# In three norms of a transformer kernel the GpSimd engine multiplies every second part by the inverse root, and the scalar engine makes the modulated row from it

## The reference, cut to what matters

```
h = x * rsqrt(mean(x^2) + eps) * g * (1 + scale) + shift
x_new = x_new + gt2 * squared_relu_mlp(h, w1, w2)
```

## Time and profile before

| | us |
|---|---|
| three runs | 1960.61, 1961.11, 1963.31 |
| median | 1961.11 |
| the profiled execution | 1964.24 |
| its span | 1962.4 |
| PE busy | 1858.6 (95%) |
| DVE busy | 1176.7 (60%) |
| ACT busy | 901.2 (46%) |
| POOL busy, 156 instructions | 103.7 (5%) |

### The profile page before, as it was taken

How to read it: one execution, slowest core, us unless ns; L and a number is a source line. 1 busy time by engine, 2 the same in 40 slices (tenths; PEclk the granted TensorE clock), 3 DMA queues, 4 the chain that set the end, 5 groups by cost and what they waited for, 6 DMA issues and landing times.

```text
span 1962.4 us, 28960 instructions
## 1 busy us (share of the span) xinstructions
PE 1858.6 (95%) x11398; PEld 1484.1 (76%) x11398; DVE 1176.7 (60%) x2039; ACT 901.2 (46%) x1552; POOL 103.7 (5%) x156
## 2 busy tenths in 40 slices
PE   7999899988999899999998999999899899999999
PEld 6889754445977554788787888888778548999999
DVE  5778732335633566578976666666743555676665
ACT  6564422115554577632235433232374576455443
POOL 0000012221000000001100000000000000000000
PEclk9999999999999999999999999999999999999999
DMA  9546799997522002155633444556533013554553
GB/s 335 182 146 220 290 397 412 413 415 284 172 86 80 22 1 86 56 181 193 208 114 132 159 160 131 190 182 205 194 108 102 22 43 108 176 190 151 183 183 130
DMA packets 199255, 345.48 MB, mean 176 GB/s; under 512 B 14096, under 2 KB 158736, under 8 KB 185936
## 3 DMA queue, kind: packets, MB, share of 16 engines
q1 hardware_dynamic: 177024, 284.88, 41.6%
q0 software_dynamic: 21952, 57.97, 8.7%
q10 hardware_dynamic: 144, 0.79, 0.1%
HBM read 392.86 MB, written 1.05 MB: 201 GB/s over the span
## 4 chain that ended last, share of the span: by engine, by line
PE 77%; DVE 9%; DMA 6%; ACT 4%; issue 2%; SPq 0%; DVEq 0%; ACTq 0%
PE PS L861 20%; PE PS L863 19%; PE PS L862 19%; PE PS L987 3%; PE PS L1236 3%; DMA SCR<-in_w_exp 3%; DVE JUNK L2219 2%; PE PS L1005 2%; DMA ring<-in_w_exp 2%; PE PS L1022 2%; DVE CR L1912 2%; PE PS L1219 1%; PE PS L1264 1%; DMA LC<-in_w_mod 1%; PE PS L993 1%
## 5 line engine op out<-in xcount | busy, mean ns | idle before, releaser
L1912 DVE TENSOR_TENSOR CR<-ring,CR 128x1024 fp32r<-128x1024 f32 x328 | 400.2, 1222 | 294.7 <-ACT CR L1457 282.6
L861 PE MATMUL PS<-HX,CR 128*128 128x256 f32 (+1 forms) x1512 | 507.7, 336 | 20.9 <-DVE HX L1961 11.4
L862 PE MATMUL PS<-HX,CR 128*128 128x256 f32 (+1 forms) x1512 | 495.6, 328 | 0.0
L863 PE MATMUL PS<-HX,CR 128*128 128x256 f32 (+1 forms) x1512 | 495.5, 328 | 0.0
L1457 ACT ACTIVATE CR<-ring 128x1024 fp32r<-128x1024 f32 x328 | 344.8, 1052 | 313.0 <-PE PS L863 312.0
L861 PEld LDWEIGHTS PS<-HX,CR 128*128 128x128 f32 x1512 | 289.9, 192 | 55.5 <-issue 28.5
L861 PE MATMUL PS<-AR,CR 128*128 128x256 f32 (+1 forms) x960 | 316.7, 330 | 6.7 <-DVE CR L1912 3.9
L862 PE MATMUL PS<-AR,CR 128*128 128x256 f32 (+1 forms) x960 | 315.8, 329 | 0.0
L863 PE MATMUL PS<-AR,CR 128*128 128x256 f32 (+1 forms) x960 | 315.8, 329 | 0.0
L862 PEld LDWEIGHTS PS<-HX,CR 128*128 128x128 f32 x1512 | 290.1, 192 | 28.8 <-issue 5.0
L863 PEld LDWEIGHTS PS<-HX,CR 128*128 128x128 f32 x1512 | 289.5, 191 | 24.4
(11 more groups left out here) (275 smaller groups left out, 2437.0 us busy)
## 6 DMA issues: line engine op xcount, KB each, us to landing
ring<-in_w_in SPq DMA_DIRECT2D x66, 1024.0 KB, 5.3
ring<-in_ffn_w SPq DMA_DIRECT2D x64, 1024.0 KB, 5.3
A<-in_w_exp SPq DMA_DIRECT2D x25, 1024.0 KB
HXW<-in_w_exp SPq DMA_DIRECT2D x25, 1024.0 KB, 18.1
LC<-in_w_mod POOLq DMA_DIRECT2D x48, 512.0 KB, 4.3
BR<-in_w_mod POOLq DMA_DIRECT2D x48, 512.0 KB, 3.6
ring<-in_w_exp SPq DMA_DIRECT2D x22, 1024.0 KB
SCR<-in_w_exp SPq DMA_DIRECT2D x22, 1024.0 KB
```

The lines of the kernel that those rows point to most:

```text
L861: pe.matmul(bank, wh, xh, start=start, stop=False, skip_group_check=skip)
L862: pe.matmul(bank, wh, xl, start=False, stop=False, skip_group_check=skip)
L863: return pe.matmul(bank, wl, xh, start=False, stop=stop, skip_group_check=skip)
L1912: dve.tensor_tensor(lo, src, hi, ALU.subtract).then_inc(lo_done, 1)
```

## The change

In B0n2, B1n1 and B1n2 every second part is made in another way. In the two norms of 16 parts the second parts are the context half of each k; in B1n2 they are the odd k.

- POOL: where = X * R (`scale_odd`, a tensor_tensor of 128 x 256), 8 + 8 + 4 instructions, all issued one behind the other once R is ready. They stand in POOL's list ahead of BR <- c_rows (B0n2) and at its end (B1n1, B1n2).
- ACT: where = where * MA + shift in place, then a wait for its own result, then HH = copy of where. For the other parts ACT is as before.
- DVE: no `scale` for these parts; `rest` is HL = where - HH, a tensor_tensor in place of a scalar_tensor_tensor.

The other norms of the program (`n_mix`, `n_pleg`, `B0n1`) are as before, and so are PE's and SP's programs.

```diff
@@ gpsimd
             for n in range(MOD_EARLY, MOD_TILES):
                 load_mod(0, n)
+            def scale_odd(T, norms, where):
+                gp.wait_ge(rstd, norms)
+                parts = [(st, k) for k in range(KD) for st in range(T // S)]
+                for st, k in parts[1::2]:
+                    at = slice(st * S, st * S + S)
+                    gp.tensor_tensor(where[:, k, at], X[:, k, at], R[:, 0, at], ALU.mult).then_inc(scaled_by_pool, 1)
+            scale_odd(2 * S, 7, NS2)
             gp.wait_ge(tile_ready, plan.tile_at["B0out7"] + 1)
             gp.dma_start(BR[:, 2 * D:4 * D], t["c_rows"]).then_inc(c_again, 16)
...
             gp.dma_start(BR[:, :], t["na_bias"][1]).then_inc(bias1_loaded, 16)
+            scale_odd(2 * S, 8, NS)
+            scale_odd(S, 9, NS2)
@@ scalar, norm_high
+                        if pooled and (k * (T // S) + st) % 2:
+                            c["pooled"] += 1
+                            act.wait_ge(scaled_by_pool, c["pooled"])
+                            act.activation(where[:, k, at], where[:, k, at], ACT.Identity, bias=shift(st, k),
+                                           scale=pooled(st, k)).then_inc(h_whole, 1)
+                            act.wait_ge(h_whole, c["pooled"])
+                            act.activation(HH[:, k, at], where[:, k, at], ACT.Copy).then_inc(norm_hi, 1)
+                            continue
@@ vector, norm_split
-                    if shift is None:
+                    if shift is None or pooled and (k * (T // S) + st) % 2:
                         ins = dve.tensor_tensor(HL[:, k, at], where[:, k, at], HH[:, k, at], ALU.subtract)
...
                 for i, part in enumerate(parts):
-                    scale(*part)
+                    if not (pooled and i % 2):
+                        scale(*part)
                     if i >= 2:
                         rest(*parts[i - 2])
```

More of the change, by code:

```diff
@@ L449, in program @@
         squares, rstd, scaled, normed = sem("squares"), sem("rstd"), sem("scaled"), sem("normed")
+        scaled_by_pool, h_whole = sem("scaled_by_pool"), sem("h_whole")
         silu_c, evac = sem("silu_c"), sem("evacuated")
@@ L1430, in _ @@
             ph = [0]
-            c = dict(step=0, squares=0, rstd=0, hn=0, hnr=0, ml=0, unit=0, gate=0, x=0, chunk=0, scaled=0, merged=0)
+            c = dict(step=0, squares=0, rstd=0, hn=0, hnr=0, ml=0, unit=0, gate=0, x=0, chunk=0, scaled=0, pooled=0, merged=0)
             def next_phase():
@@ L1488, in norm, with norm_high @@
                 inverse_root(tile, R[:, r, 0:T], inv, T, split_first=split_first).then_inc(rstd, 1)
-            def norm_high(T, shift=None, where=NS, behind={}):
+            def norm_high(T, shift=None, where=NS, behind={}, pooled=None):
                 for k in range(KD):
@@ L1780, in _ @@
                      lambda k: f"pleg{k}" if l == 0 else f"B0down{GROUPS_F - 1}_{k}", k0=0 if l else KD - 1)
-                norm_high(Tn, lambda st, k: MOD[:, l, k, st:st + 1])
+                norm_high(Tn, lambda st, k: MOD[:, l, k, st:st + 1],
+                          pooled=(lambda st, k: MA[:, 0, st, k:k + 1]) if l else None)
                 items, h0 = norm_items(l), c["hn"]
@@ L1856, in _ @@
                      lambda k: f"{L}out{min(k + 1, KD - 1)}", split_first=False)
-                norm_high(T, lambda st, k: MOD[:, l, 24 + k, st:st + 1], NS2, {4: lambda: split(f"{L}n2")})
+                norm_high(T, lambda st, k: MOD[:, l, 24 + k, st:st + 1], NS2, {4: lambda: split(f"{L}n2")},
+                          lambda st, k: MA[:, 1, st, k:k + 1])
                 if l == 0:
@@ L1942, in norm, with norm_split @@
                 c["normed"] += n
-            def norm_split(T, gain, shift=None, where=NS):
+            def norm_split(T, gain, shift=None, where=NS, pooled=False):
                 wait_rstd()
@@ L1970, in norm_split, with norm_modulated @@
                 c["normed"] += len(parts)
-            def norm_modulated(T, n, l, shift_tile, where=NS):
+            def norm_modulated(T, n, l, shift_tile, where=NS, pooled=False):
                 norm_split(T, lambda st, k: MA[:, n, st, k:k + 1],
-                           lambda st, k: MOD[:, l, shift_tile + k, st:st + 1], where)
+                           lambda st, k: MOD[:, l, shift_tile + k, st:st + 1], where, pooled)
             def attention_steps(units, L):
@@ L2439, in _ @@
                 split(f"{L}n1")
-                norm_modulated(512 if l else S, 0, l, 0)
+                norm_modulated(512 if l else S, 0, l, 0, pooled=l == 1)
                 items = norm_items(l)
@@ L2554, in _ @@
                     residual(f"{L}out{j}", j, 16)
-                norm_modulated(T, 1, l, 24, NS2)
+                norm_modulated(T, 1, l, 24, NS2, True)
                 split(f"{L}n2")
```

## The result

| | before | changed |
|---|---|---|
| median of 13 runs each, us | 1962.98 | 1967.77 |
| lowest and highest | 1960.61 to 1966.30 | 1965.49 to 1971.18 |
| the profiled execution | 1964.24 | 1969.70 |
| its span | 1962.4 | 1967.5 |

The ratio is 1.0026, with a 95% interval of 1.0019 to 1.0034: the change makes the kernel about 5.1 us slower (3.7 to 6.7). The forecast was 1962.6, +1.5 us, with 0.64 for a change within 3.9 us. The time lies in the stated range, but at the place of the rival called full alternation (1967), and the loss is beyond those 3.9 us.

A forecast was written before the change was run, and what follows sets the result against it. PE was taken to bound the kernel, only its time to the first k counting. POOL holding up DVE adds 0.57 (B0n2), 0.7 (B1n1) and about 0.3 us (B1n2): +1.5 on 1961.11 gives 1962.6, range 1959.4 to 1968.5.

The forecast's parts named there:

- full alternation: Rival in the three norms: each POOL product follows one DVE instruction and stops the next for 0.7; +5.8 us, chance 0.25.
- What bounds the kernel: Whole kernel: PE, busy 95% of the span; in the changed norms only the time to the first k is on the path.
- the -0.06 and -0.13 at the first k: First k without hindrance between engines: PE starts 0.06 us sooner in B0n2 and B1n1, 0.13 in B1n2; sum -0.25.
- ACT's steps: Pooled parts on ACT: Identity with scale 0.51, wait 0.03, copy 0.42; 1.27 us for each k, under PE's 1.36.
- The product, 0.7 us: Duration of one POOL product, taken as the middle between 0.42 us on DVE and POOL's dearest instruction, 1.00 us.
- POOL's list at no cost: Transfers behind B0n2's eight products: c_rows lands about 1069.8, still 2 us ahead of ACT's use; cost 0.
- POOL gets in only where DVE waits anyway: Likeliest case, shared port in the three norms: POOL's products run only in DVE's waits; sum +1.5 us, chance 0.45.
- ACT paces the stage and leaves DVE small waits, in which POOL's remaining products fit: Reason for taking +1.5 us as the value: remaining products fit DVE's waits, and later k have 1 us of cover.
- 0.57, 0.7 and 0.3: Forecast delay in us of PE's start on the first k in B0n2, B1n1 and B1n2, the last about 0.3.
- the condition I set for it: The alternation rival decides from a product of about 0.5 us that is served between each two DVE instructions.
- The signs I had set: In the changed profile: PE's B0n2 wait 4.6 us, not above 5.3; PE waits at k = 1 and 2 mean alternation.
- The rule of the Trainium skill that stands in the prediction: DVE instructions with two SBUF inputs contend with GpSimd instructions reading SBUF; whoever issues first keeps the shared pair until done.

The follow-up runs named there:

- product_on_dve: Changed kernel with the product X*R of every second part on DVE instead of POOL, ACT's two steps kept: ratio to the kernel before 0.9993.
- pool_last_rows_first: Changed kernel with only k = 6 and 7 pooled, POOL held until the fourth k, c_rows, LC and two modulation tiles issued first: ratio to kernel before 1.0002.
- rows_first: Changed kernel with c_rows, LC and the first two modulation tiles issued ahead of B0n2's products: ratio to the kernel before 1.0021.
- pool_last: Changed kernel with only k = 6 and 7 pooled, POOL held until the fourth k is complete: ratio to the kernel before 1.0034, repeated 1.0031.
- pool_later: Changed kernel with only k = 3 and up pooled, POOL starting when the first k is complete: ratio to the kernel before 1.0020.
- x_products_twice: Kernel before the change plus 16, 16 and 8 unused POOL products, started when R is ready in the three norms: ratio 1.0093.
- x_products_late: Kernel before the change plus 8, 8 and 4 unused POOL products started after DVE's third scale, with c_rows, LC and two modulation tiles issued first: ratio 1.0047.

## Why the prediction was right or wrong

- **The number fell into the range by its width, not by the sum.** 1962.6 was +1.5 us and the kernel lost 5.1, more than the 3.9 below which the forecast spoke of the same time. The range held the result because it reached up to the rival, which had 0.25. That is luck, as far as the value goes.
- **What bounds the kernel: right.** product_on_dve, with ACT's two steps and without POOL, is at 0.9993. Relief of DVE was tried without harm from POOL only at the end of a norm (pool_last_rows_first, 1.0002), where it is worth nothing, as forecast; the -0.06 and -0.13 at the first k were never seen alone.
- **ACT's steps: right.** 0.59 for the Identity with scale (0.51 forecast), 0.03 for the wait, 0.42 for the copy; about 1.34 us a k in place of 1.27, just under PE's 1.36. No wait of PE comes from it.
- **The product, 0.7 us: right** as a duration alone (0.73); 0.90 between DVE's instructions.
- **POOL's list at no cost: right**, with the cover as described (rows_first); pool_last showed what it costs when it is gone.
- **The failed step is "POOL gets in only where DVE waits anyway", and "ACT paces the stage and leaves DVE small waits, in which POOL's remaining products fit".** POOL does not look for gaps. From R on, each product took a turn between two DVE instructions that had no gap at all, and each turn cost 0.47 us. So the first k came 1.18, 1.08 and 1.11 us later, in place of 0.57, 0.7 and 0.3. That is 3.4 us of waits instead of 1.5. Of the other 1.7 us the traces locate 0.3 to 0.4, in the clock.
- **The rival of full alternation was the right mechanism with a wrong price.** It had the whole 0.7 as DVE's loss and so waits at k = 1 and k = 2, which are not there: with 0.47, k = 1 is ready 2.6 us behind k = 0, and PE takes 2.7. Its +1.26 for the first k is close to the 1.18, its 0.9 for B1n2 under the 1.11. That its sum of 5.8 lies near 5.1 is in part chance: its waits are 2.4 us too large, and it had nothing for what the waits leave open. I gave it 0.25; the condition I set for it (a product of about 0.5 us served between each two instructions) was met. The signs I had set would have missed it: PE's wait in B0n2 was to stay under 5.3 us and is 5.21, and alternation was to show as waits at k = 1 and k = 2.
- The rule of the Trainium skill that stands in the prediction ("SBUF — State Buffer", Who interferes with whom) was the best guide to the mechanism and should have had more than half of the chances. That the other engine is blocked for the whole of a product is not what the traces show: DVE lost 0.47 of 0.73 us.

## What to carry to other kernels

Before elementwise work goes to GpSimd, look at what DVE runs in the same microseconds: if its instructions read two SBUF tensors, each product of GpSimd costs DVE about 0.5 us, here more than the 0.40 us instruction that was taken away. Relief counts only where the engine relieved is waited for; work that must go to GpSimd belongs where the consumer lags behind by more than the stretched DVE needs, not just behind its first input (pool_later still lost 0.2%), and its transfers ahead of it in the list. Where a wait of TensorE moves by 1 us, take the granted clock of the stretch behind it into the sum.

## What the runs showed of the hardware that was not expected

- The cost of a meeting does not grow with DVE's instruction: 0.47 us on one of 0.40 and 0.48 on one of 1.22. POOL's does: a product takes 0.90 us beside the short ones and 1.72 beside the long.
- POOL's memset of 128x256 takes 0.26 us (4.12 / 16) and leaves DVE at 0.40 us apart; the residual on DVE, with one operand in PSUM, is not stretched by a product either (1.00 us for two).
- A product can also be the one that stands: 3.86 us in pool_last_rows_first, with DVE at its full pace. What decides is open.
- The time at 1.2 GHz after a wait of 4.0 us differs by some 3 us between traces (clock 0.90 over 15 us before, 0.80 in product_on_dve). Where PE gets its work in pieces, it costs about as much as the waits (x_products_twice, 8.1 and 9.2 us) or more (x_products_late, 5.9 and 3.6).
